# Selection rounds of the first attention split by query tile, with the search ahead of the reciprocal and the replacement behind it

## The chip, the cores and the metric

The kernel runs on one core of a Trainium2 chip. The metric is the device time of one execution, in microseconds. Five engines work beside each other, each with its own queue in program order: TensorE (PE), VectorE (DVE), ScalarE (ACT), GpSimd (POOL) and SyncE (SP), which issues the loads. They meet only at semaphores.

## The reference

Two models in a row are computed, with all values in fp32. The part that the change touches is the first layer's mixer, for 256 tokens: an NSA attention with 8 heads, and a DSA attention with 8 heads that lets each query see only the 64 keys with the highest index score. Cut to that:

```python
def block(qb):                       # dsa_attention
    isc = jnp.einsum('bqj,bqjs->bqs', iwb, rel)
    isc = jnp.where(spos[None, None, :] <= t[None, :, None], isc, NEG_INF)
    _, idx = lax.top_k(isc, topk)    # topk = min(256, 256 // 4) = 64
    c_sel = ckv[bi, idx]
    logits = jnp.einsum('bqhr,bqkr->bhqk', qlb, c_sel) * scale + bias
    p = masked_softmax(logits, (dist >= 0)[:, None])
```

The NSA attention has a selected and a windowed branch for each head, and at this length both are causal softmaxes over up to 256 keys; their outputs are weighted with a gate per token, head and branch.

## The kernel before, in words

The 256 queries are two tiles of 128. Scores of tile 0 take 128 columns and those of tile 1 take 256, side by side in one buffer of 384 columns (`PARTS`). A *unit* is one head and one branch with both tiles; the NSA attention has 16 units (`NSA`), the DSA attention 8. Units run through a pipeline of steps, written out by hand as one function for each engine:

- TensorE, in step s (`attention_tensor`): the logits of unit s (L1001, L1002), a projection for the DSA queries in steps 2 to 9 (L1116), two idle products of two passes each (L514), the transposes of unit s − 2 (L1037, three tiles), and the product of unit s − 3 with the values (L1132 in even units, L1137, L1138).
- VectorE, in step s (`attention_vector`): scaled logits plus bias from PSUM into `zb` (L1009 for tile 0, L1010 for tile 1), two maxima (L1012, L1014), then for unit s − 1 the reciprocal of the sums (L1237) and the product with the gates, which makes the coefficients (L1239), and behind it the selection work. After units 3, 7, 11 and 15 of the values product a head pair is rounded (L1052).
- ScalarE: the exponentials of unit s with their sums (L1020), which wait for the maxima, and copies of the transposes to SBUF (L1044).
- GpSimd (`attention_gpsimd`): each unit's exponentials times the coefficients (L1027, one instruction for each tile), behind the product L1239. The transposes of the unit wait for it (`pool.at("p", u)`).

There are four buffers for the units (NB = 4).

The selection finds the 64 highest scores of each query in 8 rounds. A round searches the 8 largest in `taken` (L1222, `max`) and replaces them by a low value (L1225, `match_replace`, which shows as a value load and a replacement), for each tile. Rounds 0 to 7 run in steps 2 to 9, both tiles in each. In step 2 the scores are copied to `taken` first (L1246), and in step 10 two operations turn `taken` into a mask (L1251, L1253). GpSimd adds the mask to the bias for the DSA units (L1288, L1289), in its queue behind the scaling of the last NSA unit. The DSA attention follows, and after it the rest of the layer.

SyncE loads weights into a ring of four slots, in the order of a list. Each load waits for its slot: for a weight, until VectorE has made its low half (L462).

Of the kernel before, what the change touches and what calls it, by code (L numbers as in the profile page):

```python
# [28 lines left out]
REPLACED = -3e38  # L29
# [219 lines left out]
def program(nc, I, out):  # L249
    ctx = ExitStack()  # L250
    with ctx:
        mem = Memory(nc)
        pe, act, vec, pool = (Signal(nc, ctx, n) for n in ("tensor", "scalar", "vector", "gpsimd"))
# [77 lines left out]
        top8 = mem.take("top8", QT, 8)  # L331
# [14 lines left out]
        isc = mem.take("isc", UC, at=ln_at)  # L346
        taken = mem.take("taken", UC, at=ln_at + UC)
# [110 lines left out]
        def lower_weights(e, c):  # L458

            high, low = weights(c)  # L460
            e.wait_ge(*act.at("high", c))
            e.tensor_tensor(low, in_ring(("w", c)), high.bitcast(F32), ALU.subtract).then_inc(*vec.up("low", c))  # L462
# [90 lines left out]
        def ada_put(e, l, j):  # L553

            n, part, half = ADA_N[l, j], j // 2, j % 2
            b = ps.of(("ada", n))
            e.wait_ge(*pe.at("ada_sum", n))
            if part in (2, 5):
                rows = gate_rows[:, part // 3, half_cols(half)]
                e.wait_ge(*landed.at(f"gate{part // 3}", l + 1))  # L560
                e.scalar_tensor_tensor(rows, b[:, :], 1.0, rows, ALU.add, ALU.add).then_inc(*vec.up("ada_put", n))
            else:
                which = {0: 0, 1: 1, 3: 2, 4: 3}[part]
                e.tensor_tensor(ada_cols[:, which, half * 4:half * 4 + 4], b[:, 0:4], col("ada_b", l * 48 + j * 4, 4),
                                ALU.add).then_inc(*vec.up("ada_put", n))
# [28 lines left out]
        PARTS = ((0, slice(0, P)), (1, slice(P, UC)))  # L594
# [409 lines left out]
        def unit_logits_vector(e, u, scale, bias0, bias1, slot_free):  # L1004
            z, st, b = z_of(u), st_of(u), ps.of(("unit", u))
            e.wait_ge(*pe.at("logits", u))
            if slot_free:
                e.wait_ge(*slot_free)
            e.scalar_tensor_tensor(z[:, 0:P], b[:, 0:P], scale, bias0, ALU.mult, ALU.add).then_inc(*vec.up("z0", u))  # L1009
            e.scalar_tensor_tensor(z[:, P:UC], b[:, P:UC], scale, bias1, ALU.mult, ALU.add).then_inc(*vec.up("z", u))  # L1010
            e.wait_ge(*vec.at("z0", u))
            e.tensor_reduce(st[:, 0:1], z[:, 0:P], AX_X, ALU.max, negate=True).then_inc(*vec.up())  # L1012
            e.wait_ge(*vec.at("z", u))
            e.tensor_reduce(st[:, 1:2], z[:, P:UC], AX_X, ALU.max, negate=True).then_inc(*vec.up("max", u))  # L1014
# [25 lines left out]
        def unit_turn_scalar(e, u, slot_free):  # L1040
            e.wait_ge(*pe.at("turn", u))
            if slot_free:
                e.wait_ge(*slot_free)
            e.activation(pT_of(u), ps.of(("turn", u))[:, 0:UC], ACT.Copy).then_inc(*act.up("pT", u))  # L1044
# [5 lines left out]
        def head_out_vector(e, i, name, stage):  # L1050
            e.wait_ge(*act.at("o_high", stage, i))
            e.tensor_tensor(oL[:, i, :], ps.of(name)[:, 0:SEQ], oH[:, i, :].bitcast(F32), ALU.subtract).then_inc(  # L1052
                *vec.up("o", stage, i))
# [42 lines left out]
        DSA0 = len(NSA)  # L1096
        BRANCH = ((k_sel, 0), (k_win, P))

        def slot_free(u, signal, name):
            return signal.at(name, u - NB) if u >= NB else None  # L1100

# [113 lines left out]
                    head_out_scalar(e, 4 + h // 2, ("heads", 4 + h // 2), "dsa")  # L1215
            round_weights(e, MLP0)

        def select_round(e, r):

            for t, c in PARTS:  # L1220
                e.wait_ge(*vec.at("taken", r - 1, t))
                e.max(top8[:, t, :], taken[:, c]).then_inc(*vec.up("top", r, t))  # L1222
            for t, c in PARTS:
                e.wait_ge(*vec.at("top", r, t))
                e.match_replace(taken[:, c], top8[:, t, :], taken[:, c], REPLACED).then_inc(*vec.up("taken", r, t))  # L1225

        def attention_vector(e):
            for step in range(len(NSA) + 3):
                if step < len(NSA):
                    h = NSA[step][0]  # L1230
                    unit_logits_vector(e, step, SCALE, bias[:, h, P:SEQ], bias[:, h, :], slot_free(step, pe, "turn"))
                u = step - 1
                if 0 <= u < len(NSA):
                    h, branch = NSA[u]
                    st = st_of(u)
                    e.wait_ge(*act.at("e", u))
                    e.reciprocal(st[:, 4:6], st[:, 2:4]).then_inc(*vec.up())  # L1237
                    e.wait_ge(*vec.now())
                    e.tensor_tensor(st[:, 4:6], st[:, 4:6], gates[:, :, 3 * h + 1 + branch], ALU.mult).then_inc(  # L1239
                        *vec.up("coef", u))  # L1240
                if step < 2:
                    lower_weights(e, 7 + step)
                elif step < 10:
                    if step == 2:
                        e.wait_ge(*pool.at("isc"))
                        e.tensor_copy(taken, isc).then_inc(*vec.up("taken", -1, 0))  # L1246
                        vec.also("taken", -1, 1)
                    select_round(e, step - 2)
                elif step == 10:
                    e.wait_ge(*vec.now())  # L1250
                    e.tensor_scalar(taken, taken, -1e38, 1.0, ALU.is_le, ALU.subtract).then_inc(*vec.up())  # L1251
                    e.wait_ge(*vec.now())
                    e.tensor_scalar(taken, taken, -NEG, None, ALU.mult).then_inc(*vec.up("mask"))  # L1253
                u = step - 3
                if u >= 0 and u % 4 == 3:
                    head_out_vector(e, u // 4, ("heads", u // 4), "nsa")
            for step in range(8 + 4):
                if step < 8:
                    s = step % 2
                    e.wait_ge(*pool.at("dbias", step))  # L1260
                    unit_logits_vector(e, DSA0 + step, SCALE, dbias[:, s, 0:P], dbias[:, s, P:UC],
                                       slot_free(DSA0 + step, pe, "turn"))
                h = step - 1
                if 0 <= h < 8:
                    st = st_of(DSA0 + h)
                    e.wait_ge(*act.at("e", DSA0 + h))
                    e.reciprocal(st[:, 4:6], st[:, 2:4]).then_inc(*vec.up("coef", DSA0 + h))
                if step < 2:
                    lower_weights(e, EV_OUT + 1 + step)
                if step == 8:  # L1270
                    lower_weights(e, EV_OUT + 3)
                h = step - 4
                if h >= 0 and h % 2:
                    head_out_vector(e, 4 + h // 2, ("heads", 4 + h // 2), "dsa")
            ada_put(e, 0, 9)
            lower_weights(e, MLP0)
# [1450 lines left out]
        def vector(e):  # L2727
            ev_vector(e)
            attention_vector(e)
            modulation(e, 1, 0, "mod", 1)  # L2730
            norm_vector(e, "y0", 0, landed.at("x_tok", QT), MLP0)
            e.wait_ge(*vec.now())
            vec.stage("mlp0")
            mlp_vector(e, "m0", MLP0, relu_tmp, BETWEEN0, {14 + t: partial(new_residual, tag="y0", ln_uses=1, t=t) for t in range(QT)})
            modulation(e, 0, 1, "mod", 2)
            norm_vector(e, "m0", 1, None, OD)
            e.wait_ge(*vec.now())
            vec.stage("od")
            diff_vector(e)
            modulation(e, 1, 2, "mod", 3)  # L2740
            norm_vector(e, "y1", 0, None, MLP1)
            e.wait_ge(*vec.now())
            vec.stage("mlp1")
            mlp_vector(e, "m1", MLP1, relu_tmp, BETWEEN1,
                       {**{6 + t: partial(new_residual, tag="y1", ln_uses=3, t=t) for t in range(QT)}, 16: meta_low_vector})
            two_norms_vector(e)
            e.wait_ge(*vec.now())
            vec.stage("two")
            axial = axial_vector(e)
            in_vector(e, axial)  # L2750
            e.wait_ge(*vec.now())
            vec.stage("delta")
            beside_axial(lambda *chunk: delta_vector(e, *chunk), axial)
            e.wait_ge(*vec.now())
            vec.stage("end")
            end_vector(e)
# [128 lines left out]
```

## Time and profile before

| | us |
|---|---|
| median of 3 runs | 1306.34 |
| lowest and highest | 1304.51, 1308.42 |
| span of the profiled execution | 1308.6 |
| TensorE busy | 1204.4 |
| VectorE busy | 824.2 |
| ScalarE busy | 614.4 |
| GpSimd busy | 63.9 |

The profiled execution has no time of its own beside its span of 1308.6 us, which reaches from its first to its last instruction. Its mean granted TensorE clock is 0.963. All times inside the profile count from the start of the span. The steps 0 to 18 of the first attention lie between about 147 and 209 us; steps 2 to 9, with the selection rounds, begin on VectorE at 161.97 us, and step 10 at 186.55.

### The profile page before, as it was taken

The numbers are of one execution on the slowest core, as the hardware profiler recorded it, in microseconds if no ns is written. First come the engines' busy times: TensorE is split into PE (matmuls) and PEld (weight loads), VectorE is DVE, ScalarE is ACT, GpSimd is POOL, SyncE is SP. The second block draws the span as 40 slices with busy tenths as digits, with TensorE's granted clock in tenths as the row PEclk, the third lists the DMA queues.
The fourth block names the chain that finished last, engine by engine and source line by source line (L and its number), as shares of the span: only waits on it lengthen the run. The fifth ranks groups of instructions, "written<-read, shape, count | busy, mean of one in ns | idle before, by whom it ended". The sixth has DMA issues, their size and how long they took to land.

```text
span 1308.6 us, 19807 instructions
## 1 busy us (share of the span) xinstructions
PE 1204.4 (92%) x8111; PEld 1070.4 (82%) x8111; DVE 824.2 (63%) x1298; ACT 614.4 (47%) x1097; POOL 63.9 (5%) x93
## 2 busy tenths in 40 slices
PE   2878999999999999889999999996789999999997
PEld 1757966788989889878999998995668887899996
DVE  7576574579998685557755447748665545544444
ACT  0431354564454455565455455365643334645543
POOL 0011055300000000000000000110000000000000
PEclk9989899999999999889999999898589999999999
DMA  9788502259999655323885651440000015456640
GB/s 351 277 294 297 196 28 65 97 181 350 365 348 339 218 167 171 116 78 118 284 272 184 215 181 37 135 153 1 1 1 17 1 65 177 134 190 192 193 162 33
DMA packets 138490, 218.76 MB, mean 167 GB/s; under 512 B 7056, under 2 KB 95504, under 8 KB 138016
## 3 DMA queue, kind: packets, MB, share of 16 engines
q1 hardware_dynamic: 138400, 217.49, 49.5%
q8 instruction: 65, 1.06, 0.3%
q14 instruction: 25, 0.20, 0.0%
HBM read 216.42 MB, written 1.05 MB: 166 GB/s over the span
## 4 chain that ended last, share of the span: by engine, by line
PE 78%; DVE 12%; ACT 5%; DMA 2%; issue 1%; POOL 1%; SPq 0%; DVEq 0%; ACTq 0%
PE bank L468 19%; PE bank L470 19%; PE bank L469 19%; PE bank L2146 2%; PE bank L2158 2%; PE bank L2154 2%; PE bank L493 2%; DVE ada_acc L537 1%; DMA ring<-ada_w 1%; PE bank L2406 1%; DMA ring<-ev_w_in 1%; DVE low L462 1%; DVE act_low L1335 1%; PE bank L1002 1%; PE bank L1037 1%
## 5 line engine op out<-in xcount | busy, mean ns | idle before, releaser
L462 DVE TENSOR_TENSOR low<-ring,high 128x2048 fp32r<-128x2048 f32 (+1 forms) x139 | 317.7, 2287 | 255.4 <-ACT high L456 254.8
L456 ACT ACTIVATE high<-ring 128x2048 fp32r<-128x2048 f32 (+1 forms) x139 | 264.5, 1905 | 262.0 <-PE bank L470 173.8
L468 PE MATMUL bank<-act_high,high 128*128 128x256 f32 (+1 forms) x1112 | 321.7, 289 | 6.0 <-DVE act_low L1335 6.0
L470 PE MATMUL bank<-act_high,low 128*128 128x256 f32 (+1 forms) x1112 | 316.4, 285 | 0.0
L469 PE MATMUL bank<-act_low,high 128*128 128x256 f32 (+1 forms) x1112 | 316.4, 285 | 0.0
L468 PE MATMUL bank<-high,act_high 128*128 128x512 f32 (+1 forms) x632 | 232.7, 368 | 2.5 <-DVE act_low L2651 1.8
L470 PE MATMUL bank<-high,act_low 128*128 128x512 f32 (+1 forms) x632 | 230.7, 365 | 0.0
L469 PE MATMUL bank<-low,act_high 128*128 128x512 f32 (+1 forms) x632 | 230.6, 365 | 0.0
L468 PEld LDWEIGHTS bank<-act_high,high 128*128 128x128 f32 x1112 | 214.0, 192 | 11.4 <-DVE act_low L1335 6.8
L469 PEld LDWEIGHTS bank<-act_low,high 128*128 128x128 f32 x1112 | 214.1, 193 | 2.6 <-issue 1.7
L470 PEld LDWEIGHTS bank<-act_high,low 128*128 128x128 f32 x1112 | 214.0, 192 | 0.0
L468 PEld LDWEIGHTS bank<-high,act_high 128*128 128x128 f32 x632 | 119.1, 188 | 21.8 <-DVE act_low L2651 2.0
L470 PEld LDWEIGHTS bank<-high,act_low 128*128 128x128 f32 x632 | 119.0, 188 | 20.4
L469 PEld LDWEIGHTS bank<-low,act_high 128*128 128x128 f32 x632 | 119.1, 189 | 17.9
L537 DVE SCALAR_TENSOR_TENSOR ada_acc<-ring,c_act,ada_acc 128x512 f32<-128x512 f32 x168 | 126.6, 753 | 8.6 <-DMA ring<-ada_w 1.1
L1020 ACT ACTIVATE zb<-zb,ust 128x128 f32<-128x128 f32 x80 | 35.8, 448 | 51.2 <-DVE ust L1014 50.6
L508 PE MATMUL bank<-cols 128*128 128x128 f32 x438 | 54.2, 283 | 0.0
L508 PEld LDWEIGHTS bank<-cols 128*128 128x128 f32 x438 | 52.8, 200 | 0.3
L550 PE MATMUL bank<-ones,ada_acc 128*128 128x1 f32 x128 | 19.0, 270 | 26.0 <-DVE ada_acc L537 26.0
L550 PEld LDWEIGHTS bank<-ones,ada_acc 128*128 128x128 f32 x128 | 19.4, 225 | 27.3 <-DVE ada_acc L537 13.6
L1027 POOL TENSOR_SCALAR zb<-zb,ust 128x128 f32<-128x128 f32 (+1 forms) x48 | 36.3, 769 | 70.4 <-DVE ust L1239 57.7
L2075 POOL MEMSET conv<- 128x24 f32 x1 | 0.1, 123 | 564.1 <-DVE x_tok L1857 564.1
(467 smaller groups left out, 1502.2 us busy)
## 6 DMA issues: line engine op xcount, KB each, us to landing
ring<-mlp_w SPq DMA_DIRECT2D x64, 1024.0 KB, 5.9
ring<-ada_w SPq DMA_DIRECT2D x48, 1024.0 KB, 7.2
ring<-w_up SPq DMA_DIRECT2D x16, 1024.0 KB, 5.6
ring<-w_down SPq DMA_DIRECT2D x16, 1024.0 KB, 4.9
ring<-od_w_in SPq DMA_DIRECT2D x12, 1024.0 KB, 5.2
ring<-w_in SPq DMA_DIRECT2D x11, 1024.0 KB, 5.3
ring<-ev_w_in SPq DMA_DIRECT2D x8, 1024.0 KB, 7.4
ring<-ev_w_out SPq DMA_DIRECT2D x4, 1024.0 KB, 8.3
```

The costliest lines, as they stand in the source:

```text
L456: e.activation(weights(c)[0], in_ring(("w", c)), ACT.Copy).then_inc(*act.up("high", c))
L462: e.tensor_tensor(low, in_ring(("w", c)), high.bitcast(F32), ALU.subtract).then_inc(*vec.up("low", c))
L468: e.matmul(out_, ah, bh, start=start, stop=False)
L469: e.matmul(out_, ah, bl, start=False, stop=False)
L470: return e.matmul(out_, al, bh, start=False, stop=stop)
L493: last = e.matmul(out_, src[:, k, toks], w[:, k, c0:c0 + n_cols], start=k == 0, stop=k == n - 1)
L508: m = e.matmul(b[:, 0:P], ident, ident, start=True, stop=True)
L537: e.scalar_tensor_tensor(acc, w_[:, k, :], c_, acc, ALU.mult, ALU.add).then_inc(*vec.up())
L550: m = e.matmul(b[:, i:i + 1], acc[:, i * P:(i + 1) * P], ones[:, 0:1], start=True, stop=True)
L1020: x = e.activation(z[:, c], z[:, c], ACT.Exp, bias=st[:, t:t + 1], accum_out=st[:, 2 + t:3 + t])
L1027: x = e.tensor_scalar(z[:, c], z[:, c], st[:, 4 + t:5 + t], None, ALU.mult)
L2146: m = e.matmul(o, B["aT"][0:C, h, 0:C], B["x"][0:C, h, 0:C], start=True, stop=True)
```

## The change

Rounds 0 to 2 keep a step each, for both tiles (steps 2 to 4). Rounds 3 to 7 are split: one tile in a step, tile 0 in odd steps and tile 1 in even ones, over steps 5 to 14. In each of these steps the searches come ahead of the reciprocal, and the replacements come between the reciprocal and the product with the gates. The copy of the scores moves from step 2 to step 1, ahead of the reciprocal there, and the two mask operations from step 10 to step 15. No instruction is added or taken away.

```diff
+        SELECTS = {2: ((0, 0), (0, 1)), 3: ((1, 0), (1, 1)), 4: ((2, 0), (2, 1))}
+        for i in range(10):
+            SELECTS[5 + i] = ((3 + i // 2, i % 2),)
...
-        def select_round(e, r):
-
-            for t, c in PARTS:
-                e.wait_ge(*vec.at("taken", r - 1, t))
-                e.max(top8[:, t, :], taken[:, c]).then_inc(*vec.up("top", r, t))
-            for t, c in PARTS:
-                e.wait_ge(*vec.at("top", r, t))
-                e.match_replace(taken[:, c], top8[:, t, :], taken[:, c], REPLACED).then_inc(*vec.up("taken", r, t))
+        def select_largest(e, r, t):
+            c = PARTS[t][1]
+            e.wait_ge(*vec.at("taken", r - 1, t))
+            e.max(top8[:, t, :], taken[:, c]).then_inc(*vec.up("top", r, t))
+
+        def select_replace(e, r, t):
+            c = PARTS[t][1]
+            e.wait_ge(*vec.at("top", r, t))
+            e.match_replace(taken[:, c], top8[:, t, :], taken[:, c], REPLACED).then_inc(*vec.up("taken", r, t))
 
         def attention_vector(e):
             for step in range(len(NSA) + 3):
                 if step < len(NSA):
                     h = NSA[step][0]
                     unit_logits_vector(e, step, SCALE, bias[:, h, P:SEQ], bias[:, h, :], slot_free(step, pe, "turn"))
+                if step == 1:
+                    e.wait_ge(*pool.at("isc"))
+                    e.tensor_copy(taken, isc).then_inc(*vec.up("taken", -1, 0))
+                    vec.also("taken", -1, 1)
+                rounds = SELECTS.get(step, ())
+                for r, t in rounds:
+                    select_largest(e, r, t)
                 u = step - 1
                 if 0 <= u < len(NSA):
                     h, branch = NSA[u]
                     st = st_of(u)
                     e.wait_ge(*act.at("e", u))
                     e.reciprocal(st[:, 4:6], st[:, 2:4]).then_inc(*vec.up())
+                    for r, t in rounds:
+                        select_replace(e, r, t)
                     e.wait_ge(*vec.now())
                     e.tensor_tensor(st[:, 4:6], st[:, 4:6], gates[:, :, 3 * h + 1 + branch], ALU.mult).then_inc(
                         *vec.up("coef", u))
                 if step < 2:
                     lower_weights(e, 7 + step)
-                elif step < 10:
-                    if step == 2:
-                        e.wait_ge(*pool.at("isc"))
-                        e.tensor_copy(taken, isc).then_inc(*vec.up("taken", -1, 0))
-                        vec.also("taken", -1, 1)
-                    select_round(e, step - 2)
-                elif step == 10:
-                    e.wait_ge(*vec.now())
+                if step == 15:
+                    e.wait_ge(*vec.at("taken", 7, 0))
+                    e.wait_ge(*vec.at("taken", 7, 1))
                     e.tensor_scalar(taken, taken, -1e38, 1.0, ALU.is_le, ALU.subtract).then_inc(*vec.up())
```

## Rows read from the trace of the kernel before

**Rows 1.** The page: each engine's busy time, and the chain that ended last.

```profile
PE 1204.4 (92%) x8111; PEld 1070.4 (82%) x8111; DVE 824.2 (63%) x1298; ACT 614.4 (47%) x1097; POOL 63.9 (5%) x93
...
PE 78%; DVE 12%; ACT 5%; DMA 2%; issue 1%; POOL 1%; SPq 0%; DVEq 0%; ACTq 0%
```

**Rows 2.** Windows: length, busy time of each engine, granted clock, DMA share, GB/s.

```profile
163.00:190.00 27.00, 26.88 (x154) 17.73 (x153) 22.72 (x106) 14.94 (x55) 13.84 (x18) 1.00 0.11 37
190.00:205.00 15.00, 14.39 (x79) 9.17 (x80) 7.26 (x33) 7.07 (x26) 7.78 (x11) 1.00 0.01 3
...
225.00:230.00 5.00, 3.93 (x24) 3.16 (x24) 1.78 (x8) 3.28 (x13) 5.00 (x9) 1.00 0.46 161
...
300.00:400.00 100.00, 100.00 (x637) 89.93 (x636) 92.36 (x101) 46.18 (x43) 0.00 (x0) 1.00 1.01 353
```

**Rows 3.** Timeline of VectorE, step 5: start, duration, instruction, idle before it.

```profile
170.91 0.29 DVE L1009 SCALAR_TENSOR_TENSOR zb<-bank,bias 128x128 f32<-128x128 f32 x1 [0.46 <-PE bank L1002]
...
171.97 0.15 DVE L1237 RECIPROCAL ust<-ust 128x2 f32<-128x2 f32 x1
172.16 0.16 DVE L1239 TENSOR_TENSOR ust<-ust,gates 128x2 f32<-128x2 f32 x1
172.24 0.61 DVE L1222 MAX8 top<-taken 128x8 f32<-128x128 f32 x2
172.77 0.07 DVE L1225 MATCH_VALUE_LOAD taken<-top,taken 128x8 f32 x1
...
173.09 0.41 DVE L1225 MATCH_REPLACE8 taken<-top,taken 128x256 f32<-128x256 f32 x1
174.10 0.29 DVE L1009 SCALAR_TENSOR_TENSOR zb<-bank,bias 128x128 f32<-128x128 f32 x1 [0.60 <-PE bank L1002]
```

**Rows 4.** Groups by line and shape, VectorE: busy time, mean ns of one.

```profile
L1222 DVE MAX8 top<-taken 128x8 f32<-128x256 f32 x8 | 3.3, 409 | 0.0
...
L1222 DVE MAX8 top<-taken 128x8 f32<-128x128 f32 x8 | 2.3, 287 | 0.0
```

**Rows 5.** Timeline of GpSimd: steps 2, 4, 5, 10, 12 and 15.

```profile
163.47 1.54 POOL L1027 TENSOR_SCALAR zb<-zb,ust 128x128 f32<-128x128 f32 x2 [5.27 <-DVE ust L1239]
...
169.37 1.50 POOL L1027 TENSOR_SCALAR zb<-zb,ust 128x128 f32<-128x128 f32 x2 [1.51 <-DVE ust L1239]
172.42 1.50 POOL L1027 TENSOR_SCALAR zb<-zb,ust 128x128 f32<-128x128 f32 x2 [1.54 <-DVE ust L1239]
...
188.06 1.78 POOL L1027 TENSOR_SCALAR zb<-zb,ust 128x128 f32<-128x128 f32 x2 [1.68 <-DVE ust L1239]
...
194.20 1.50 POOL L1027 TENSOR_SCALAR zb<-zb,ust 128x128 f32<-128x128 f32 x2 [1.47 <-DVE ust L1239]
...
203.22 2.98 POOL L1027 TENSOR_SCALAR zb<-zb,ust 128x128 f32<-128x128 f32 x4 [1.67 <-DVE ust L1239]
```

**Rows 6.** Timeline of TensorE: transposes behind those scalings, idle products ahead of two.

```profile
165.07 0.55 PE L1037 MATMUL bank<-cols,zb 128*128 128x128 f32 x3
...
171.36 0.49 PE L1037 MATMUL bank<-cols,zb 128*128 128x128 f32 x3
...
174.54 0.49 PE L1037 MATMUL bank<-cols,zb 128*128 128x128 f32 x3
...
189.06 0.71 PE L514 MATMUL bank<-cols 128*128 128x128 f32 x4
189.90 0.55 PE L1037 MATMUL bank<-cols,zb 128*128 128x128 f32 x3
...
195.75 0.55 PE L1037 MATMUL bank<-cols,zb 128*128 128x128 f32 x3
...
203.45 0.71 PE L514 MATMUL bank<-cols 128*128 128x128 f32 x4
204.78 0.55 PE L1037 MATMUL bank<-cols,zb 128*128 128x128 f32 x3 [0.61 <-POOL zb L1027]
```

**Rows 7.** Waits of SyncE's queue, 155 to 225 us: total, times, longest.

```profile
SPq L2831 <- DVE zb L1009: 54.7, 1, 54.7
```

## Prediction

> **What bounds the kernel now.** I read the page first: the share of each engine and the chain that ended last. TensorE is busy for 92% of the span and carries 78% of the chain, VectorE 12% of it [rows 1]. The change touches only the first attention, so the windows come next. From 163 to 190 us, where all but the first steps of the selection run, TensorE is busy 26.88 of 27.00 us at a granted clock of 1.00, VectorE 22.72 us; from 190 to 205 us TensorE has 14.39 of 15.00 and VectorE only 7.26 [rows 2]. TensorE is the bound of this stage. VectorE has room in both halves, and more in the second.
>
> The third view is VectorE's timeline of one step with a round (step 5). It starts the logits at 170.91 after waiting 0.46 us for TensorE's L1002, comes to the reciprocal at 171.97 and to the coefficient product L1239 at 172.16, and only then does the selection: 172.24 to about 173.42. The next logits start at 174.10, after another wait of 0.60 us for TensorE [rows 3]. So the round lies behind the last thing that anybody waits for, and it ends before the next thing can start.
>
> Who waits for the product L1239? GpSimd's scaling L1027, two instructions that take 1.50 us together, and behind them TensorE's transposes L1037 of the same unit [rows 5, 6]. This is the race that decides the case: POOL against the queue of TensorE. In step 4 POOL ends at 169.37 + 1.50 = 170.87 and the transposes start at 171.36. Steps 6 and 8 repeat it, each with a gap of 0.48 us. In step 12 they are 195.70 and 195.75, which is no slack at all. In step 10 POOL ends at 189.84 and the transposes start at 189.90, later than the 189.06 + 0.55 = 189.61 at which they would stand without a wait (0.55 us is what four passes of idle product take ahead of them in every step), and in step 15 they start at 204.78 instead of 203.45 + 0.55 = 204.00 [rows 5, 6]. From POOL's end to the start of a transpose that waited it takes 0.06 us, and the three transposes then take 0.55 instead of 0.49 us [rows 6]. A free margin is therefore the gap less 0.12 us: 0.37 in step 4, 0.36 in steps 6 and 8, and 0 in steps 2 (165.01 and 165.07), 12 and 14, whose transposes show 0.55 us as well; step 14 repeats step 12. Stalls now: about 0.06 us in each of these three, 0.29 + 0.06 = 0.35 in step 10, 0.78 + 0.06 = 0.84 in step 15.
>
> **The change part by part.** The forty-eight selection records (16 searches, 16 value loads, 16 replacements) stay the same. What moves is their place: each step's searches now stand in front of the reciprocal and its replacements between reciprocal and product. Everything GpSimd waits for comes later by their time.
>
> *Delay of the product.* VectorE's records overlap by some 0.08 us: the two searches last 0.287 and 0.409 us by themselves [rows 4] and from 172.24 to 172.77 = 0.53 together, and from the first value load at 172.77 to the end of the second replacement at 173.50 it is 0.65 us, its last 0.08 left out as overlap [rows 3]. In front of the product I count full rounds as 0.53 + 0.65 = 1.18, with 0.02 us more because the product now stands right behind the replacement: 1.20 us. A single round on tile 0 is 0.20 + 0.25 + 0.02 = 0.47, on tile 1 0.33 + 0.40 + 0.02 = 0.75. The lower bound leaves the 0.02 out; the upper one has no overlap: 1.53, 0.64 and 0.90 us.
>
> The Trainium skill says otherwise of the overlap: VectorE: DVE Perf Modes, section "The DRAIN you can't avoid", has the next operation start only when the pipe has emptied. These rows show starts 0.08 us ahead of the previous record's end, and by the page's rule the delays would be those of my upper bound; by the rows they are the ones I take.
>
> *What a delay costs.* A step's stall is the delay less the margin, less the stall of the step before, since that stall moves TensorE's next transposes too but not the logits that VectorE starts from. So two stalls in a row share. Odd steps from 3 have wide margins (in step 5 POOL ends at 172.42 + 1.50 = 173.92 and the transposes start at 174.54, a gap of 0.62; the three others up to step 9 have 0.62 to 0.88) [rows 5, 6]. They carry either the 0.47 us of tile 0 or, in step 3, a full round behind the large stall of step 2: no cost there. The even steps pay:
> Step 2: 1.20 (margin 0). Step 4: 1.20 − 0.37 = 0.83. Steps 6 and 8: 0.75 − 0.36 = 0.39 each, 0.78 together. Step 10: the stall is 0.75 + 0.07 = 0.82 after 0.35, so 0.47. Steps 12 and 14: 0.75 each, 1.50. Sum 4.78 us.
>
> *The mask.* Its two operations leave step 10 for step 15. In step 10 GpSimd's pair took 1.78 us instead of 1.50, with the mask operations at the same time [rows 5]. I expect those 0.28 us in step 15 instead. Step 15 stalls 0.84 now; it inherits the 0.82 of step 14 and gets the 0.28: 0.84 + 0.28 − 0.82 = 0.30, a gain of 0.54. That the mask is ready some 19 us later costs nothing: GpSimd's first bias sum comes behind the scaling of unit 15 in its queue anyway, and the mask would be done by about 208 against a scaling that ends near 210 (203.22 + 2.98 = 206.20 now, and 4 us more) [rows 5].
>
> The Trainium skill, SBUF — State Buffer, section "Who interferes with whom", says that a tensor_scalar may take the port pair shared with GpSimd and block it for a whole instruction. By that rule, the trace agrees (1.78 against 1.50 us), and a longest possible block would be the two mask operations' own 0.36 and 0.41 us.
>
> *The copy of the scores* (0.35 us) goes from step 2 to step 1. VectorE waits for ScalarE's rounding of weights right behind that step, and TensorE has a whole projection ahead of unit 0's transposes: nothing. If that cover were gone, it would cost 0.4 us. Step 3's logits start some 0.3 us earlier without it; they are not what TensorE waits for. VectorE itself does the same work in steps 2 to 4, about 2.5 us of a step of 3.0, and less from step 5 on: nothing. ScalarE's exponential waits for the maximum L1014, which no selection work precedes: nothing. No DMA moves: SyncE waits for one release over this whole stage, 54.7 us, and the loads start again only behind the second attention's first weights [rows 7]. So whatever the stage loses is lost at the end too; the stretch from 300 to 400 us runs its DMA at a share of 1.01, but begins with the ring as full as now, only later [rows 2].
>
> Sum: 4.78 − 0.54 = 4.24 us, +0.32%. The profiled execution has a span of 1308.6 us, 2.3 above the median of the three times; the sum is a difference and goes on the median: 1306.34 + 4.24 = 1310.6 us. Bounds: with delays 0.02 shorter and margins 0.06 wider, 1.12 + 0.75 + 2 × 0.31 + 0.45 + 2 × 0.67 − 0.39 = 3.9; without any overlap 1.53 + 1.16 + 2 × 0.54 + 0.62 + 2 × 0.90 − 0.69 = 5.5. The real cost can still be smaller if stalls overlap more than I count.
>
> **Rivals.**
> *A, hidden.* The delays are swallowed: margins are wider than I read them, or the 4.2 us come back in a later stage that the DMA bounds. For it: the DMA share of 1.01 from 300 us on [rows 2], and that GpSimd is idle half of each step. Against it: step 12 has 0.05 us between POOL and TensorE [rows 5, 6]. It decides where even steps have more than 0.75 us of margin, or where those loads start independently of this stage. 1306.3 us, within a microsecond or two. Half of the sum hidden gives 1308.5.
> *B, a gain.* VectorE paced steps 2 to 9 with its rounds, and spreading them helps. From the transposes at 171.36 to those at 189.90 six steps pass in 18.54 us, 3.03 each without the 0.35 of stall, and the next two in 5.85, 2.93 each [rows 6]. At that rate the eight would take 0.8 us less, and the stalls of steps 10 and 15 would go, 1.2: 1304.3 us at best. It needs VectorE to be what the logits wait for; the rows show the reverse, with 0.46 and 0.60 us of waiting for TensorE in a step [rows 3]. It decides if VectorE never waits there.
> *C, the clock.* More holes in TensorE's work pull the granted clock to the lower level (1.2 GHz) for part of the stage. Against it: from 225 to 230 us TensorE is busy for 3.93 of 5.00 us, with a hole of 1.1, at a clock of 1.00 [rows 2], and the new stalls are 0.4 to 1.25 us of a step. If it came, ten microseconds at half the clock would do the work of five and add five: 1315.6.
>
> **How the numbers follow.** About 0.3% (3.9 us) is what a measurement of this kernel can tell from no change, and my sum lies just above it. My forecast, a loss of 3.9 to 5.5 us give or take 1 us for the medians (three runs of the kernel before lie 3.9 apart), has a chance of 0.68; A, in full or in half, 0.20; B 0.07; C 0.05. The range of 80% reaches down to A's 1306.3 and up over the upper bound, 1306.3 + 5.5 = 1311.8 and a microsecond for the median: 1306.3 to 1313.0. The forecast's own part is spread around the bound, some 0.48 over and 0.20 under it; with C slower has 0.53. A falls within; of B I give 0.05 to faster by over 0.3%, which would need more than it names. Faster 0.05, same 0.42, slower 0.53.
>
> **What would show it.** In the changed kernel the product's start minus the reciprocal's should go from 0.19 to about 0.9 us in steps 2 to 4, and 0.5 to 0.65 in the later ones, and the reciprocal should stand 0.2 to 0.5 us later behind L1014. TensorE should show waits for POOL L1027 ahead of L1037 in steps 2, 4, 6, 8, 10, 12 and 14, near 1.2, 0.8, 0.3, 0.3, 0.8, 0.8 and 0.8 us, and the one at the end should shrink from 0.61 to under 0.3. GpSimd's 1.78 should be gone from step 10. The first matmul of the second attention (209.03 now) should be 4.2 us later, and later stages should keep this distance. I am wrong if VectorE's logits start earlier relative to TensorE's, if the waits appear in odd steps too, or if the distance at 209 us is not there at the end.

## The result, and the profile after

The changed kernel is slower: 1314.17 us median of 5 (1310.81 to 1316.48) against 1306.34, ratio 1.0053 with a 95% interval of 1.0037 to 1.0070. Two more sets of executions beside other kernels gave 1.0053 (1.0028 to 1.0078) and 1.0056 (1.0035 to 1.0077). The forecast was 1310.6, with a range that ended at 1313.0: the sign is right, the size is not. The loss is 6.9 us by the ratio (7.8 between the two medians) instead of 4.2.

The page of the changed kernel, engines and the chain that ended last:

```profile
span 1314.7 us, 19808 instructions
...
PE 1208.7 (92%) x8111; PEld 1069.1 (81%) x8111; DVE 824.5 (63%) x1298; ACT 614.8 (47%) x1097; POOL 63.9 (5%) x93
...
PE 70%; DVE 16%; ACT 6%; DMA 5%; issue 2%; POOL 1%; SPq 0%; DVEq 0%; ACTq 0%
```

The work is the same, only TensorE's records are 4 us longer in sum [rows 1]. The shares of the chain have moved too (TensorE from 78 to 70%, VectorE from 12 to 16%, DMA from 2 to 5%); nothing below rests on them. The stage itself says where. Its windows in the changed kernel (length, busy time of PE, PEld, DVE, ACT, POOL, granted clock, DMA share, GB/s), with the cuts at the places where the clock changes:

```profile
157.00:163.00 6.00, 5.01 (x29) 3.56 (x28) 5.43 (x25) 3.34 (x13) 1.50 (x2) 0.97 0.55 175
163.00:180.00 17.00, 17.00 (x56) 10.35 (x55) 5.95 (x28) 4.03 (x14) 4.51 (x6) 0.51 0.00 1
180.00:203.00 23.00, 21.54 (x119) 13.91 (x118) 15.25 (x69) 11.44 (x44) 10.53 (x14) 1.00 0.00 1
203.00:210.00 7.00, 7.00 (x23) 4.19 (x22) 2.32 (x10) 2.20 (x9) 2.53 (x4) 0.54 0.01 4
210.00:218.50 8.50, 8.21 (x45) 5.30 (x45) 3.00 (x11) 2.68 (x8) 5.82 (x9) 0.98 0.00 0
```

The third column from the end is the reading: the granted clock is at its lower level, 1.2 GHz, for 17 us from just before 163 on and again for nearly 7 us from 203.4 on. Before, it was 1.00 throughout [rows 2]. A TensorE that is "busy 17.00 of 17.00" there does 56 matmul records, where the filled kernel below does 98 in the same 17 us.

Steps are counted here and below as VectorE's: the product in step s belongs to unit s − 1, and so do the transposes that wait for it. VectorE in step 2 of the changed kernel, to be read against rows 3:

```profile
158.02 0.29 DVE L1009 SCALAR_TENSOR_TENSOR zb<-bank,bias 128x128 f32<-128x128 f32 x1 [0.50 <-PE bank L1002]
...
159.08 0.61 DVE L1225 MAX8 top<-taken 128x8 f32<-128x128 f32 x2
159.60 0.15 DVE L1249 RECIPROCAL ust<-ust 128x2 f32<-128x2 f32 x1
159.67 0.07 DVE L1230 MATCH_VALUE_LOAD taken<-top,taken 128x8 f32 x1
...
159.99 0.41 DVE L1230 MATCH_REPLACE8 taken<-top,taken 128x256 f32<-128x256 f32 x1
160.43 0.16 DVE L1253 TENSOR_TENSOR ust<-ust,gates 128x2 f32<-128x2 f32 x1
```

From the logits to the product it is 2.41 us, where it was 172.16 − 170.91 = 1.25 [rows 3]: a delay of 1.16. In step 5 (172.67 to 174.44) and step 6 (178.55 to 180.59) it is 0.52 and 0.79. A kernel below with the same order and the clock at 1.00 throughout (holes filled) has 1.16, 0.51 and 0.78 in these steps.

The transposes of the changed kernel that waited for GpSimd, with the idle time ahead of each in brackets, in TensorE's timeline:

```profile
162.25 0.60 PE L1037 MATMUL bank<-cols,zb 128*128 128x128 f32 x3 [0.99 <-POOL zb L1027]
...
189.20 0.55 PE L1037 MATMUL bank<-cols,zb 128*128 128x128 f32 x3 [0.20 <-POOL zb L1027]
...
195.85 0.55 PE L1037 MATMUL bank<-cols,zb 128*128 128x128 f32 x3 [0.64 <-POOL zb L1027]
...
202.49 0.55 PE L1037 MATMUL bank<-cols,zb 128*128 128x128 f32 x3 [0.63 <-POOL zb L1027]
...
214.28 0.55 PE L1037 MATMUL bank<-cols,zb 128*128 128x128 f32 x3 [0.29 <-POOL zb L1027]
```

These are steps 2, 8, 10, 12 and 15. Steps 4, 6 and 14 do not wait: they lie in, or right behind, stretches in which TensorE is slow, and GpSimd is in time for a slow TensorE.

As a measure for all kernels below I take the stretch from the logits of step 1 (154.22 in the kernel before) to the first logits of the second attention (209.03) [for the clock there, rows 2]: 54.81 us before, 150.27 to 218.53 = 68.26 after. The profiled execution as a whole is only 6.1 us longer, because it reached the stretch 4 us earlier (the granted clock from 100 to 150 us was 0.93 against 0.86) and caught up 3.4 us later, most of it from 800 to 1000 us, where its clock was 0.89 against 0.86. One execution does not give the loss to better than a few microseconds; the stretch inside one does.

### The profile page after: what moved, and what is told of

Same layout as the page of the kernel before. It is cut to its first block, busy times and chain, and to the rows that moved or that the text cites. A ratio compares the mean times of both kernels' runs of the same rounds, so it can differ in the third digit from the quotient of the medians.

```text
span 1314.7 us, 19808 instructions
## 1 busy us (share of the span) xinstructions
PE 1208.7 (92%) x8111; PEld 1069.1 (81%) x8111; DVE 824.5 (63%) x1298; ACT 614.8 (47%) x1097; POOL 63.9 (5%) x93
## 3 DMA queue, kind: packets, MB, share of 16 engines
q8 instruction: 65, 1.06, 0.3%
## 4 chain that ended last, share of the span: by engine, by line
PE 70%; DVE 16%; ACT 6%; DMA 5%; issue 2%; POOL 1%; SPq 0%; DVEq 0%; ACTq 0%
PE bank L468 17%; PE bank L470 16%; PE bank L469 16%; DVE ada_acc L537 3%; DVE low L462 2%; PE bank L2155 2%; PE bank L2167 2%; DMA ring<-mlp_w 2%; PE bank L2163 2%; PE bank L493 2%; DMA ring<-ada_w 1%; ACT high L456 1%; PE bank L2415 1%; DMA ring<-ev_w_in 1%; PE bank L1002 1%
## 5 line engine op out<-in xcount | busy, mean ns | idle before, releaser
L462 DVE TENSOR_TENSOR low<-ring,high 128x2048 fp32r<-128x2048 f32 (+1 forms) x139 | 317.7, 2287 | 256.4 <-ACT high L456 256.1
L1009 DVE SCALAR_TENSOR_TENSOR zb<-bank,bias 128x128 f32<-128x128 f32 x32 | 9.2, 288 | 35.0 <-PE bank L1002 35.0
```

## The experiments

Nine runs split the loss into its parts, and three see what the stage can give. Each edit is shown against the kernel that its heading names.

**Rounds behind the product again.** Against the changed kernel:

```diff
-                for r, t in rounds:
-                    select_largest(e, r, t)
...
-                    for r, t in rounds:
-                        select_replace(e, r, t)
...
                         *vec.up("coef", u))
+                for r, t in rounds:
+                    select_largest(e, r, t)
+                for r, t in rounds:
+                    select_replace(e, r, t)
```

> The changed kernel's split schedule, but with the searches and replacements of a step both behind the product L1239, as they stood before the change. Theory 1 (the loss is the delay of the product, first as waits of TensorE and then as a lower clock that the waits bring): no product is late, so no new wait and no fall of the clock in this attention: within 1.5 us of the kernel before, 1306 us. Theory 2 (waits alone, the clock is chance): the same here. Theory 3 (the split or the moved copy and mask cost by themselves): stays near 1314.

Measured: ratio 1.0001 (0.9988 to 1.0014), stretch 54.66 us, clock 1.00. The split, the moved copy and the moved mask cost nothing; all of the loss comes from what stands ahead of the product. Theory 3 is out. The wait in front of unit 14's transposes grew from 0.61 to 0.78 us, the mask's collision with GpSimd: 0.17, where I had 0.28 (GpSimd's four instructions there take 3.15 instead of 2.98 us).

**Holes filled with idle products.** Against the changed kernel:

```diff
+        FILL = {1: 4, 3: 2, 9: 2, 11: 2, 13: 2}
...
             if by is pool:
-                idle_products(e, b, 2)
+                idle_products(e, b, 2 + FILL.get(u, 0))
```

> The changed kernel with two to four more idle products ahead of the transposes of units 1, 3, 9, 11 and 13, those that wait longest for GpSimd. They take 0.5 to 1.1 us of TensorE's time each, inside waits of 0.7 to 1.2 us. Theory 1: the holes are filled, the clock stays at 1.00 from 157 us to the second attention, and what is left is the waits, 4 us: 1310 to 1311. Theory 2: the products change nothing, or add: 1314 or more. If the products did not fit in the waits they would add up to 3 us.

`FILL` names units; unit 1 is the one of step 2, and two products are four passes. Measured: ratio 1.0037 (1.0024 to 1.0051). The trace has the same late products and no fall. Its windows, with columns as above:

```profile
157.00:163.00 6.00, 6.00 (x46) 5.28 (x45) 3.59 (x7) 2.64 (x5) 1.20 (x2) 1.00 0.39 145
163.00:180.00 17.00, 16.58 (x98) 11.32 (x97) 11.42 (x55) 8.31 (x31) 7.51 (x10) 1.00 0.17 54
180.00:213.00 33.00, 32.26 (x181) 20.78 (x179) 18.63 (x82) 14.56 (x52) 17.36 (x24) 1.00 0.01 1
```

And the filled wait of step 2: twelve passes instead of four, and the transposes start 1.71 us behind the first (0.55 without a wait).

```profile
164.22 1.60 PE L514 MATMUL bank<-cols 128*128 128x128 f32 x12
165.93 0.55 PE L1039 MATMUL bank<-cols,zb 128*128 128x128 f32 x3
```

The stretch is 153.95 to 212.97 = 59.02 us, 4.21 longer than before. This is the sum of the waits with the clock out of the way; I had worked out 4.24. The sum does not hide errors that cancel. From the logits of one step to those of the next, this trace is longer than that of the kernel before by 1.14 us behind step 2, 0.80 behind step 4, 0.42 and 0.41 behind steps 6 and 8, 0.50 and 0.79 behind steps 10 and 12, and by 0.18 in the rest, which holds steps 14 and 15. Worked out were 1.20, 0.83, 0.39 and 0.39, 0.47 and 0.75, and 0.75 − 0.54 = 0.21.

**All rounds whole, around the reciprocal.** Against the changed kernel:

```diff
-        SELECTS = {2: ((0, 0), (0, 1)), 3: ((1, 0), (1, 1)), 4: ((2, 0), (2, 1))}
-        for i in range(10):
-            SELECTS[5 + i] = ((3 + i // 2, i % 2),)
+        SELECTS = {2 + r: ((r, 0), (r, 1)) for r in range(8)}
...
-                if step == 15:
+                if step == 10:
```

> All eight rounds whole in steps 2 to 9 and the mask in step 10, as before the change, but searches ahead of the reciprocal and replacements ahead of the product, as in the change. Every product of steps 2 to 9 is 1.2 us late. Waits: 1.2 us in step 2 and 0.83 in steps 4, 6 and 8, the odd steps in between give theirs back: 3.7 us, 1310.0 without the clock. Theory 1: larger holes than in the changed kernel, so the clock falls at the latest in step 4 and the time is 1313 or more. Theory 2: 1310. Theory 3: about 1306, since nothing is split.

Measured: ratio 1.0040 (1.0024 to 1.0057), 1313.27 us median. The stretch is 64.66 us with a window of

```profile
163.00:180.00 17.00, 17.00 (x55) 10.50 (x55) 6.61 (x32) 4.03 (x15) 4.52 (x6) 0.50 0.00 1
```

So the order costs about as much without the split as with it (3.7 us of waits were expected here and 4.2 there, and the two intervals overlap), and the fall comes in the same place.

**Only the later rounds around the reciprocal**, and, in the next set, **only the first three**. Against the changed kernel, the one and the other:

```diff
-                rounds = SELECTS.get(step, ())
+                rounds = SELECTS.get(step, ()) if step >= 5 else ()
+                late = SELECTS.get(step, ()) if step < 5 else ()
...
-                rounds = SELECTS.get(step, ())
+                rounds = SELECTS.get(step, ()) if step < 5 else ()
+                late = SELECTS.get(step, ()) if step >= 5 else ()
```

with `late` searched and replaced behind the product in both.

> The changed kernel with rounds 0 to 2 (steps 2 to 4) behind the product; rounds 3 to 7 stay around the reciprocal. Theory 1: the waits of steps 2 and 4 go, 2.0 us, and with them the first and longest fall of the clock (163 to 180 us); waits of 2.2 us stay, and a fall near step 14 may: 1308.5 to 1311. Theory 2: 1312, the measured 1314 less 2.0. Theory 3: 1314.

> The changed kernel with only rounds 0 to 2 around the reciprocal, and rounds 3 to 7 behind the product. Waits: 1.20 in step 2 and 0.83 in step 4, 2.0 us in all; the 1 us hole of step 2 and the fall of the clock behind it stay possible. Theory 1: 1309.3 where the clock holds, 1312 to 1314 where it falls, median between; together with the run that had only the later rounds around the reciprocal (1.0020) it adds up to the whole loss. Theory 2: 1309.3, spread as before.

Measured: 1.0020 (1.0004 to 1.0036) and 1.0030 (1.0014 to 1.0047). Together they lose 0.50%, against 0.53 to 0.56% for the whole. The stretch of the first is 57.09 us at a clock of 1.00 throughout: 2.28 over the kernel before, where the waits of these steps were worked out at 2.2. The second has 60.55, 5.7 over, of which the waits are 2.0; its window behind the 1 us hole of step 2 says where the rest is:

```profile
163.00:172.00 9.00, 9.00 (x30) 5.66 (x29) 2.98 (x14) 2.48 (x9) 3.00 (x4) 0.52 0.00 0
172.00:180.00 8.00, 8.00 (x44) 5.25 (x43) 4.59 (x20) 3.55 (x13) 3.00 (x4) 0.90 0.01 2
```

**The changed kernel twice more, the filled one once more, and the first three filled.** The last edit is against the kernel with only rounds 0 to 2 around the reciprocal:

```diff
+        FILL = {1: 4, 3: 2}
...
-                idle_products(e, b, 2)
+                idle_products(e, b, 2 + FILL.get(u, 0))
```

> The changed kernel itself, once more, for a second trace of it and more times. Theory 1 (4 us of waits, and in some executions a fall of the clock that they bring): ratio 1.004 to 1.006; where the trace has the clock at 1.00 from 157 us on, the second attention starts 59.0 us behind the first projection-step logits (154.22 to 209.03 = 54.8 before), where it has fallen, up to 68. Theory 2 (waits alone, and something in the rest of the kernel for the other 2.7 us): 59 us in this stretch with a later stage longer than before.

> The changed kernel once more, beside the filled ones on the same chip. Theory 1 (waits, and falls of the clock that the holes bring in part of the executions): ratio 1.0053 as twice before, mean clock 0.002 below that of the kernel before. Theory 2 (waits alone): its ratio and the filled kernel's come out the same, near 1.0045.

> The changed kernel with idle products in its holes, once more. Theory 1: ratio 1.0033 to 1.004, the mean clock level with the kernel before, and the trace at a clock of 1.00 from 155 us to the second attention, 59.0 us long as in its first trace. Theory 2: the same ratio as the changed kernel beside it; a fall of the clock in this trace as well would speak against theory 1.

> Only rounds 0 to 2 around the reciprocal, as in the earlier run at ratio 1.003, plus four idle products ahead of unit 1's transposes and two ahead of unit 3's, inside the waits. Theory 1: the clock stays at 1.00, waits of 2.0 us are left: ratio 1.0015, and 56.8 us from the first logits after the projection to the second attention against 60.5 without the products. Theory 2: 1.003 again, or a little more for the added products.

Measured: the changed kernel 1.0053 and 1.0056, as said; the filled one 1.0015 (0.9999 to 1.0031) beside the 1.0056, with a stretch of 59.01 us at a clock of 1.00; the first three filled 1.0015 (0.9999 to 1.0032, not clear of the 1.0030 without the products), with a stretch of 56.62 us (54.81 and 2.0 of waits is 56.8) at 1.00, against 60.55 unfilled. The two more traces of the changed kernel have 68.24 us, with both falls, and 61.44, with one short one. Its windows:

```profile
163.00:172.00 9.00, 8.02 (x28) 4.95 (x26) 4.44 (x22) 3.38 (x12) 3.67 (x6) 0.63 0.12 41
172.00:180.00 8.00, 7.99 (x48) 5.17 (x46) 4.60 (x21) 3.53 (x13) 3.26 (x5) 0.99 0.01 2
180.00:213.50 33.50, 31.23 (x169) 19.71 (x169) 19.22 (x84) 14.56 (x52) 17.48 (x25) 1.00 0.00 1
```

So the fall differs from one execution to the next. Each execution's mean granted clock is in the results, and this settles how much it is on average: 0.9643 over the 18 executions of the changed kernel (standard error 0.0007), 0.9674 over the 18 of the filled one (0.0005), 0.9670 over 84 of the kernel before. The other kernels fall in line: 0.9643 and 0.9644 with the hole of step 2 open (all rounds whole, first three around), 0.9662 to 0.9670 with it filled or absent (first three filled, rounds behind, later rounds only). A mean that is 0.0027 lower over 1312 us is 3.5 us of work at full clock. The mean times are 1314.5, 1311.1 and 1307.5 us: 3.4 between changed and filled (standard error 0.9), 3.6 between filled and before (0.7). The three traces of the changed kernel lose more than this mean against the filled one, 9.2, 9.2 and 2.4 us in the stretch; the 18 executions are the better measure.

**The product ahead of the logits.** Against the kernel before, `attention_vector` alone: the reciprocal and the product of unit s − 1 now open step s.

```diff
         def attention_vector(e):
             for step in range(len(NSA) + 3):
+                u = step - 1
+                if 0 <= u < len(NSA):
+                    ...
+                    e.reciprocal(st[:, 4:6], st[:, 2:4]).then_inc(*vec.up())
+                    e.wait_ge(*vec.now())
+                    e.tensor_tensor(st[:, 4:6], st[:, 4:6], gates[:, :, 3 * h + 1 + branch], ALU.mult).then_inc(
+                        *vec.up("coef", u))
                 if step < len(NSA):
```

> The kernel before, with reciprocal and product of unit s-1 ahead of the logits of unit s on VectorE, in the time in which it waits for TensorE. The product comes 1 us earlier. The stalls of steps 10 and 15 (0.35 and 0.84 us) and the 0.06 us of three others should go: 1.3 us faster, 1305.0 (ratio 0.999). If ScalarE's exponentials come too late for that, VectorE's logits wait for them and the time stays or grows.

Measured: 0.9994 (0.9978 to 1.0011), which cannot be told from no change; the stretch is 53.99 us, 0.82 shorter. The stalls of the kernel before add up to 1.32 us in its steps (0.07, 0.35, 0.06 and 0.84). In steps 2 to 15 they are gone: the transposes stand 0.54 or 0.55 us behind their idle products, also in steps 11 to 13, where VectorE waits 1.06 us for ScalarE's exponentials. What is left, 0.50 us, stands at the end of the stretch, behind unit 15, in VectorE's, GpSimd's and TensorE's timelines:

```profile
198.51 0.42 DVE L1052 TENSOR_TENSOR act_low<-bank,act_high 128x256 fp32r<-128x256 f32 x1 [1.70 <-ACT act_high L1048]
...
199.12 0.29 DVE L1009 SCALAR_TENSOR_TENSOR zb<-bank,bias 128x128 f32<-128x128 f32 x1
...
201.51 0.16 DVE L1236 TENSOR_TENSOR ust<-ust,gates 128x2 f32<-128x2 f32 x1
...
201.77 1.50 POOL L1027 TENSOR_SCALAR zb<-zb,ust 128x128 f32<-128x128 f32 x2 [0.97 <-DVE ust L1236]
...
201.71 0.65 PE L1137 MATMUL bank<-pT,v_sw 128*64 128x256 f32 x2 [0.16 <-ACT pT L1044]
...
202.50 0.71 PE L514 MATMUL bank<-cols 128*128 128x128 f32 x4
203.33 0.55 PE L1037 MATMUL bank<-cols,zb 128*128 128x128 f32 x3
```

From unit 15's logits to its product it is 201.51 − 199.12 = 2.39 us, as it was before (2.38), since the product needs this unit's own exponentials; and the logits themselves stand behind the rounding of a head pair (L1052) and the product of unit 14. GpSimd ends at 203.27 and the transposes start at 203.33, 0.28 us later than they would, and take 0.06 us longer; with the 0.16 us for ScalarE's copy this is the 0.50.

**The same without idle products, and repaired.** Against the changed kernel, besides the moved product and the rounds behind the logits:

```diff
-            if by is pool:
-                idle_products(e, b, 2)
+            if by is pool and u >= DSA0:
+                idle_products(e, b, 2)
```

> Reciprocal and product ahead of the logits as in the run beside it, the split schedule of the change with its rounds behind, and no idle products in the first attention. TensorE no longer waits for GpSimd there, so the 0.55 us of idle product a step are work for nothing: 16 steps give up to 8.8 us. If the clock holds at 1.00: 1297 to 1300. If the clock falls in the stage (TensorE now has less work a step than the chain of VectorE and ScalarE takes, about 2.4 us, and holes come back): 1302 to 1310.

`DSA0` is the first unit of the second attention, 16. Measured: 0.9988 (0.9970 to 1.0007), stretch 52.16 us. It wins 2.7 us in the stretch and loses part of it at its end, where two holes stand and the clock falls (its mean over 12 executions is 0.9645):

```profile
196.42 0.52 PE L1037 MATMUL bank<-cols,zb 128*128 128x128 f32 x3 [1.57 <-POOL zb L1027]
...
198.88 0.87 PE L1037 MATMUL bank<-cols,zb 128*128 128x128 f32 x3 [0.84 <-POOL zb L1027]
```

```profile
195.00:205.00 10.00, 7.51 (x25) 4.54 (x26) 2.20 (x8) 2.61 (x8) 4.97 (x8) 0.66 0.01 2
```

The repair, against that kernel (`head_out_vector` besides moves from the end of a step behind the next step's product):

```diff
-            if by is pool and u >= DSA0:
-                idle_products(e, b, 2)
+            if by is pool and u >= DSA0 - 2:
+                idle_products(e, b, 4 if u == DSA0 - 2 else 2)
```

> The lean kernel (product ahead of the logits, split rounds behind, no idle products) with two repairs of what its trace showed: four idle products ahead of unit 14's transposes and two ahead of unit 15's, where it waited 1.6 and 0.8 us and the clock fell, and the rounding of a head pair behind the product instead of ahead of it, where it held the product back by 1 us in steps 7, 11 and 15. If both work: clock at 1.00, stage 3 us shorter than in the lean kernel's 52.2: median 1301 to 1303, ratio 0.996. If ScalarE's queue sets the step in any case (2.47 us), only the clock's part comes: 0.9975.

Measured: 1303.15 us median against 1307.75, ratio 0.9961 (0.9945 to 0.9976): 5 us faster than the kernel before, and the only one of all here that beats it beyond its interval. The stretch is 49.14 us at a clock of 1.00:

```profile
157.00:180.00 23.00, 22.82 (x127) 14.45 (x127) 20.30 (x83) 12.86 (x49) 11.95 (x16) 1.00 0.15 47
180.00:201.00 21.00, 19.68 (x103) 11.64 (x103) 13.79 (x58) 10.75 (x39) 12.78 (x19) 1.00 0.00 1
```

## Why the prediction was wrong, point by point

The step that failed is the clock, three points down; what stands ahead of it held.

*The bound and the race.* Right. TensorE sets this stage, and it is GpSimd's scaling, behind the product, that it runs into. With the rounds behind the product nothing is lost (1.0001).

*The delay of the product.* Right: 1.16, 0.52 and 0.79 us measured for 1.20, 0.47 and 0.75. VectorE's records overlap as read from rows 3, not as by the upper bound. The prediction set against this the sentence of the Trainium skill, VectorE: DVE Perf Modes, section "The DRAIN you can't avoid", that the next operation starts only when the pipe is empty; by that sentence alone step 2 would have been 1.53 us late, and it was 1.16. The same section goes on that a next operation that is not held starts earlier, which the prediction left out, so the rows do not contradict the section as a whole.

*The cost of the delays.* Right, and better than one may expect of it: 2.28 us for the steps from 5 on (2.2 worked out) and 4.21 for all (4.24) in the traces in which the clock stayed at 1.00. That odd steps give nothing and even ones pay shows in the list of waits, and the terms came out one by one in the filled kernel. The stall of step 15 went from 0.84 to 0.23 us there (its transposes stand 0.72 us behind the idle products, 0.55 without a wait, and take 0.06 us longer), for 0.30 worked out. The wait of 0.29 us that the first trace of the changed kernel shows in step 15 stands behind a step 14 at the lower clock and is no measure of this term.

*The mask.* Its collision was sized too large, 0.28 for a measured 0.17 us. With 0.17 the term for step 15 would have been 0.19, for the 0.23 measured.

*The copy, and the stages behind.* Right. The copy costs nothing (1.0001 with the rounds behind). Nothing of the stretch is given back in the stages that load: a low half of a weight (L462) that starts at 753.00 us in the kernel before starts at 756.83 in the filled one, 3.8 later, where the filled one was 3.9 behind at the start of the second attention. In the times this can be seen only roughly: the kernels whose clock held lost 2.6 us (1.0020) for 2.28 in the stretch, and 2.0 and 4.8 (1.0015 and 1.0037) for 4.2.

*The clock.* This is the step that failed. The prediction put it as rival C, "more holes in TensorE's work pull the granted clock to the lower level", gave it 0.05, and argued against it with one window of the kernel before, in which a hole of 1.1 us left the clock at 1.00 [rows 2]. The hole of step 2 does pull it down. At its place all five traces that leave it open show the fall (three of the changed kernel, the unsplit one, the one with only the first three rounds around), and none of the five does that fill it or do not have it (twice filled, first three filled, later rounds only, rounds behind). The products in the holes change nothing else: VectorE's and GpSimd's times are as late with them as without. In the mean over executions the lower clock takes 3.4 to 3.5 us (standard error about 1), nearly as much as the waits. The forecast's 4.2 and these 3.4 are 7.6, for 6.9 to 7.3 measured. The means over executions give the same from measured parts: 3.6 for the waits and 3.4 for the clock, 7.0. C's price, 1315.6, was the forecast's 1310.6 and 5 us for the clock, and it came nearer than the forecast; but C was held apart as a rival with 0.05, so that the forecast had no term for the clock at all. The window that was held against C was read rightly, and it was no single case: the same hole of 1.08 or 1.09 us stands in the second attention of all fourteen traces, with a clock of 1.00 from 220 to 300 us in each. It says nothing of a hole in another place. TensorE's timeline in the kernel before, and then in the changed one:

```profile
225.79 0.55 PE L1037 MATMUL bank<-cols,zb 128*128 128x128 f32 x3 [1.09 <-POOL zb L1027]
```

```profile
235.31 0.55 PE L1037 MATMUL bank<-cols,zb 128*128 128x128 f32 x3 [1.09 <-POOL zb L1027]
```

The Trainium skill, TensorE: Matmul & The Clock Gate, section "HAM oscillation — how this bites in real kernels", tells of a kernel whose waits sent the clock down again and again, and puts the lower clock's cost beside that of the waits. The runs here agree in kind, with waits much shorter than those of its example: 0.51 of the clock over 17 us behind a wait of 0.99.

*Rivals A and B.* Neither happened. Nothing was hidden (4.21 us of delay in the stretch of the filled kernel), and VectorE did not pace the early steps: the kernel with the split rounds behind the product is no faster.

*What stays open.* Why the hole of 1.09 us in the second attention leaves the clock at 1.00 in every trace and the hole of 0.99 us in step 2 in none that has it, why holes of 0.63 us in steps 10 to 14 come with a fall in two traces of the changed kernel and with none in the third nor in the kernel with the later rounds only, and what makes the length of a fall differ (some 7 us of the lower level in one trace, 10 in another and 17 in three, in the first place). No run here separates the hole's own length from the work around it.

## What to carry to other kernels

Before work is put ahead of an instruction, ask who waits for that instruction, not whether its engine has room: VectorE waited for TensorE in each step, and yet the work ahead of the product reached TensorE through GpSimd: 1.14 of 1.16 us in step 2, which had no margin, and nothing in the odd steps, which had one. Margins from the timeline (the releaser's end to the waiter's start, less what a waiting start shows) gave the sum of waits, 4.24 us worked out and 4.21 measured, and each term of it, to a tenth of a microsecond. And where new holes appear in TensorE's queue, count them as waits and add a term for the clock, with a chance of its own, instead of a rival that leaves the sum as it is; idle products inside the wait tell the two apart. No row of the kernel before gives the size of that term.

## What the runs showed of the hardware that was not expected

A hole of 0.98 or 0.99 us in an otherwise full TensorE was followed by 7 to 17 us at the lower level of its clock in all five traces that have it, and TensorE then shows 17.00 of 17.00 us busy; one of 1.09 us in another place was followed by none in fourteen. While the clock is low the waits that brought it disappear (none between 162.25 and 189.20 us in the first trace of the changed kernel), so a count of waits in such a trace understates the cause: TensorE's recorded waits for GpSimd in the stage are 2.7 us in the two traces with long falls and 3.3 in the one with a short fall. Six idle products in the holes of steps 2 and 4 cost no time in the trace (56.62 us for 56.8 worked out without them) and took 3.9 us off the stretch (60.55 to 56.62). Where no wait covers them they cost their time: a step of TensorE is 0.5 us shorter without its pair (3.12 for 3.62 us behind step 2, in the kernel without idle products and in the one with the early product alone). With fourteen of the sixteen pairs gone, the product early and the rounding moved, the stretch went from 54.81 to 49.14 us at a clock of 1.00; no run separates these three.
